# An expert stage rewritten: who rounds the weights, how rows come and go, and where the two choices are summed

## The reference

```
for e in range(N_EXPERTS):
    he = silu(t @ exp_w1[e]) * (t @ exp_w3[e])
    y = y + comb[:, e:e + 1] * (he @ exp_w2[e])
```

## Time and profile before

| | us (or as given) |
|---|---|
| median of 3 runs (3298.52 to 3305.92) | 3304.67 |
| the profiled execution | 3304.96 |
| its span, first to last instruction | 3303.2 |
| DMA traffic | 445.87 MB |
| busy PE / DVE / POOL / ACT | 2738.0 / 1634.0 / 1004.3 / 897.0 |

### The profile page before, as it was taken

The page is one execution under the profiler, slowest core; times in us unless marked ns, Lnnn a source line. Parts: engine busy times, 40 slices in busy tenths (PEclk is TensorE's granted clock), DMA queues, the critical chain, the costliest instruction groups (busy, mean ns, idle before and its releaser), DMA issues. The chain is left out here.

```text
span 3303.2 us, 34922 instructions
## 1 busy us (share of the span) xinstructions
PE 2738.0 (83%) x11986; PEld 2043.3 (62%) x11986; DVE 1634.0 (49%) x1921; ACT 897.0 (27%) x1435; POOL 1004.3 (30%) x743
## 2 busy tenths in 40 slices
PE   5898997999976688619899699979999968588882
PEld 4897555767666566517655355547777757467772
DVE  4394341222134778561166454433564353688884
ACT  3012331000021333230133344422133221234441
POOL 1243222222121656313000233312322211457662
PEclk8898898999987799859799799989999988699996
DMA  2110112111041899864222233221111131699999
GB/s 85 40 45 20 35 27 63 38 51 51 6 154 65 322 339 352 313 219 153 83 58 58 75 81 78 78 63 45 51 39 37 32 136 77 226 361 366 367 356 356
DMA packets 240805, 445.87 MB, mean 135 GB/s; under 512 B 36696, under 2 KB 155816, under 8 KB 232776
## 3 DMA queue, kind: packets, MB, share of 16 engines
q1 hardware_dynamic: 219400, 367.07, 33.2%
q0 software_dynamic: 12960, 47.19, 3.8%
q10 hardware_dynamic: 8352, 30.41, 2.3%
HBM read 349.87 MB, written 90.31 MB: 133 GB/s over the span
## 5 line engine op out<-in xcount | busy, mean ns | idle before, releaser
L1795 DVE TENSOR_TENSOR moe_run_w_low<-moe_run_w,moe_run_w_high 128x2048 fp32r<-128x2048 f32 x174 | 456.0, 2628 | 87.0 <-POOL moe_run_w_high L1655 86.9
L1655 POOL CAST moe_run_w_high<-moe_run_w 128x2048 fp32r<-128x2048 f32 x116 | 285.8, 2471 | 217.5 <-DMA moe_run_w<-w_up 104.4
L134 PE MATMUL rnn_ps<-uT_again_high,rnn_w_high 128*128 128x512 f32 x512 | 205.1, 401 | 35.9 <-POOL rnn_w_low L147 19.9
L134 PE MATMUL rnn_ps<-uT_again_low,rnn_w_high 128*128 128x512 f32 x512 | 202.3, 395 | 0.0
L134 PE MATMUL rnn_ps<-uT_again_high,rnn_w_low 128*128 128x512 f32 x512 | 202.3, 395 | 0.0
L1684 PE MATMUL moe_run_up<-moe_run_w_high,moe_run_xT_high 128*128 128x512 f32 x464 | 199.9, 431 | 0.0
L1684 PE MATMUL moe_run_up<-moe_run_w_low,moe_run_xT_high 128*128 128x512 f32 x464 | 192.4, 415 | 0.0
L1684 PE MATMUL moe_run_up<-moe_run_w_high,moe_run_xT_low 128*128 128x512 f32 x464 | 191.9, 414 | 0.0
L1670 PE MATMUL moe_run_turn<-all_ident,moe_run_x 128*128 128x128 f32 x464 | 78.2, 321 | 131.2 <-DMA moe_run_x<-v,moe_run_idx 131.0
L134 PE MATMUL merge_gates<-uT_high,merge_wg_high 128*128 128x512 f32 x384 | 170.8, 445 | 17.4 <-POOL merge_wg_low L147 17.4
L1200 DVE TENSOR_TENSOR merge_gated<-merge_branch,merge_gate 128x512 f32<-128x512 f32 x48 | 33.2, 691 | 304.0 <-ACT merge_gate L1185 304.0
(11 more groups left out here) (440 smaller groups left out, 6779.5 us busy)
## 6 DMA issues: line engine op xcount, KB each, us to landing
moe_run_w<-exp_w SPq DMA_DIRECT2D x96, 512.0 KB, 8.5
moe_run_w<-w_gate SPq DMA_DIRECT2D x68, 512.0 KB, 7.0
moe_run_w<-w_up SPq DMA_DIRECT2D x68, 512.0 KB, 8.5
moe_run_w<-w_down SPq DMA_DIRECT2D x34, 1024.0 KB, 7.1
moe_y<-moe_run_y ACTq DMA_DIRECT2D x58, 512.0 KB, 7.1
moe_run_w<-exp_w SPq DMA_DIRECT2D x24, 1024.0 KB, 7.7
rnn_raw<-w_in SPq DMA_DIRECT2D x32, 512.0 KB, 3.9
moe_y<-moe_run_zero SPq DMA_DIRECT2D x26, 512.0 KB, 8.2
```

What stands on the lines that cost most here:

```text
L134: last = pe.matmul(out, a, b, start=(k == 0), stop=(k == n - 1))
L1655: pool.tensor_copy(hi[p][j][:], raw[p][j][:]).then_inc(s_hi[j], 1)
L1795: dve.tensor_tensor(lo[p][j][:], raw[p][j][:], hi[p][j][:].bitcast(F32), ALU.subtract).then_inc(s_lo[j], 1)
```

## The change

ACT now rounds w0 and w1 too (`round_up`), so ACT makes all high parts. Its order over block b becomes round_up(b+2, w0), round_middle(b), round_rows(b+2), round_up(b+2, w1), gate(b+1), round_down(b+1), copy_results(b). The first pass is written out, the others loop.

POOL keeps the indirect DMAs alone. It gathers block b+3 as soon as the rows of b+1 are turned, and scatters the results of block b: each result row goes to row (choice x 1024 + token) of `y_d`, which now has 2048 rows. ACT issues no store. Empty places carry an index outside the bounds, in gather and scatter, and those rows are left out; the two row buffers are cleared once at the start, and POOL waits for that before the first gather. The zero fill of unused blocks is gone.

The combination moves into `run_experts`. The tiles of h are loaded into the raw weight tiles of w0 and w1 behind the last blocks, the results are loaded as plain contiguous tiles, all 16 of them into the high and low weight tiles, once both last scatters have landed; sums, norm and stores follow as before. `route_tokens` gains a few small DVE operations and loses `slots`.

```diff
                 for k, oh in enumerate((oh1, oh2)):
...
-                    own(dve.tensor_copy(r["slots"][:, k, :], sl[:]))
...
                     own(TT(of_block[k][:], table(b_id[:], NB), wide(blk[:], NB), ALU.is_equal))
-                    TT(of_block[k][:], of_block[k][:].bitcast(F32), wide(t_id[:], NB), ALU.mult).then_inc(s_hot, 1)
+                    own(TS(sl[:], t_id[:], (k - 2.0) * S, None, ALU.add))
+                    TT(of_block[k][:], of_block[k][:].bitcast(F32), wide(sl[:], NB), ALU.mult).then_inc(s_hot, 1)
...
                 own(dve.tensor_copy(r["passes"][:], pf[:]))
+                own(dve.memset(r["token"][:, NB:], S))
                 dve.wait_ge(s_ids, 1)
-                dve.tensor_copy(r["token"][:], ps_id[:, 0:NB])
+                own(TS(choice[:], ps_id[:, 0:NB], 2.0 * S, None, ALU.add))
+                own(dve.tensor_copy(r["choice"][:], choice[:]))
+                own(TS(second[:], choice[:], float(S), -float(S), ALU.is_ge, ALU.mult))
+                own(TT(choice[:], choice[:], second[:], ALU.add))
+                dve.tensor_copy(r["token"][:, 0:NB], choice[:])
...
         x = [st.sb(f"x{p}", [P, D]) for p in range(2)]
...
+
+        def rows_of(tiles):
...
+        parts = [q.bitcast(F32) for q in rows_of([hi[p][j] for p in range(2) for j in range(3)] + [lo[0][0], lo[0][1]])]
+        yk = [parts[2 * t:2 * t + 2] for t in range(NT)]
         turn, hturn = st.banks("turn", 2), st.ps("hturn")
         up, down = st.banks("up", 2), st.banks("down", 2)
 
...
-                    sp.sem_inc(s_fill, 16)
                 in_order(sp, load)
                 n = more(sp)
-                sp.wait_ge(s_zero, 1)
-                with sp.Fori(n + 1, NB // 2 + 1) as i:
-                    for p in range(2):
-                        sp.dma_start(y_d[bass.ds((2 * i + p) * P, P), :], zero[:]).then_inc(s_fill, 16)
-                sp.wait_ge(s_fill, 16 * (NB + 2))
+                if g_row is not None:
+                    sp.dma_start(g[:], g_row.to_broadcast((P, D))).then_inc(s_g, 16)
+                for t in range(NT):
+                    if t % 2 == 0:
+                        sp.wait_ge(s_lo[t // 2 % 2], 2 * n + 1 + t // 4)
+                    sp.dma_start(h[t], h_d[t * P:(t + 1) * P, :]).then_inc(s_h[t], 16)
+                for p in range(2):
+                    sp.wait_ge(s_st[p], 16 * n + 16)
+                for t in range(NT):
+                    for k in range(2):
+                        at = k * S + t * P
+                        sp.dma_start(yk[t][k], y_d[at:at + P, :]).then_inc(s_yk[t], 16)
+                for t in range(NT):
+                    if g_row is not None:
+                        sp.wait_ge(s_out, t + 1)
+                    else:
+                        sp.wait_ge(s_sum, 2 * t + 2)
+                    sp.dma_start(out_d[t * P:(t + 1) * P, :], h[t]).then_inc(s_kept, 16)
+                sp.wait_ge(s_kept, 16 * NT)
...
             @block.gpsimd
             def _(pool):
-                def gather_and_round(i, p, first):
-                    b = 2 * i + p
-                    if not first:
-                        pool.wait_ge(s_turn, 2 * b - 2)
-                        pool.sem_inc(s_go, 1)
+                def gather(b, p):
                     pool.tensor_copy(idx[p][:], r["token"][:, bass.ds(b, 1)]).then_inc(s_idx, 1)
                     pool.wait_ge(s_idx, b + 1)
                     pool.sem_inc(s_go, 1)
                     pool.indirect_dma_start(
                         out=x[p][:], out_offset=None, in_=v_d,
-                        in_offset=bass.IndirectOffsetOnAxis(ap=idx[p][:, 0:1], axis=0)).then_inc(s_x[p], 16)
-                    for j, s_used in enumerate((s_half, s_up)):
-                        pool.wait_ge(s_raw[p][j], 32 * i + 32)
-                        if not first:
-                            pool.wait_ge(s_used, b - 1)
+                        in_offset=bass.IndirectOffsetOnAxis(ap=idx[p][:, 0:1], axis=0),
+                        bounds_check=S - 1, oob_is_err=False).then_inc(s_x[p], 16)
+
+                def scatter(i, p):
+                    b = 2 * i + p
+                    pool.wait_ge(s_y, 2 * b + 2 + Y0)
+                    pool.sem_inc(s_go, 1)
+                    pool.tensor_copy(to[p][:], r["choice"][:, bass.ds(b, 1)]).then_inc(s_to, 1)
+                    pool.wait_ge(s_to, b + 1)
+                    pool.sem_inc(s_go, 1)
+                    pool.indirect_dma_start(
+                        out=y_d, out_offset=bass.IndirectOffsetOnAxis(ap=to[p][:, 0:1], axis=0),
+                        in_=y[p][:], in_offset=None,
+                        bounds_check=2 * S - 1, oob_is_err=False).then_inc(s_st[p], 16)
+
+                pool.wait_ge(s_clear, 2)
+                gather(0, 0)
+                gather(1, 1)
+                pool.wait_ge(s_turn, 2)
+                gather(2, 0)
+                n = more(pool)
+                with pool.Fori(0, n) as i:
+                    for p in range(2):
+                        b = 2 * i + p + 3
+                        pool.wait_ge(s_turn, 2 * b - 2)
                         pool.sem_inc(s_go, 1)
-                        pool.tensor_copy(hi[p][j][:], raw[p][j][:]).then_inc(s_hi[j], 1)
-                in_order(pool, gather_and_round)
+                        gather(b, 1 - p)
+                        scatter(i, p)
+                for p in range(2):
+                    scatter(n, p)
+                pool.wait_ge(s_x[0], 16 * n + 32)
+                pool.sem_inc(s_go, 1)
...
             @block.scalar
             def _(act):
                 act.sem_inc(s_y, Y0)
-                for p in range(2):
-                    act.sem_inc(s_st[p], ST0)
+
+                def round_up(i, p, j, first=False):
+                    act.wait_ge(s_raw[p][j], 32 * i + 32)
+                    if not first:
+                        act.wait_ge((s_half, s_up)[j], 2 * i + p - 1)
+                    act.copy(hi[p][j][:], raw[p][j][:]).then_inc(s_hi[j], 1)
...
-                def store(i, p):
+                def copy_results(i, p, first=False):
                     b = 2 * i + p
-                    act.wait_ge(s_st[p], 16 * i + ST0)
+                    if not first:
+                        act.wait_ge(s_st[p], 16 * i)
                     for h, (a, z) in enumerate(HALVES):
                         act.wait_ge(s_down, 2 * b + h + 1 + DOWN0)
                         act.copy(y[p][:, a:z], down[h][:]).then_inc(s_y, 1)
-                    act.wait_ge(s_y, 2 * b + 2 + Y0)
-                    act.dma_start(y_d[bass.ds(b * P, P), :], y[p][:]).then_inc(s_st[p], 16)
-
+
+                round_up(0, 0, 0, True)
                 round_rows(0, 0, True)
+                round_up(0, 0, 1, True)
                 round_rows(0, 1, True)
+                round_up(0, 1, 0, True)
+                round_up(0, 1, 1, True)
                 round_down(0, 0, True)
                 gate(0, 0, True)
                 n = more(act)
-                with act.Fori(0, n) as i:
+                def one_pass(i, first=False):
                     for p in range(2):
                         nxt = (i + p, 1 - p)
-                        round_down(*nxt)
+                        round_up(i + 1, p, 0)
                         round_middle(i, p)
                         round_rows(i + 1, p)
+                        round_up(i + 1, p, 1)
                         gate(*nxt)
-                        store(i, p)
+                        round_down(*nxt)
+                        copy_results(i, p, first)
+
+                one_pass(0, True)
+                with act.Fori(1, n) as i:
+                    one_pass(i)
                 round_down(n, 1)
                 round_middle(n, 0)
                 gate(n, 1)
-                store(n, 0)
+                copy_results(n, 0)
                 round_middle(n, 1)
-                store(n, 1)
-                for p in range(2):
-                    act.wait_ge(s_st[p], 16 * n + 16 + ST0)
-                    act.sem_inc(s_end, 1)
+                copy_results(n, 1)
+                if g_row is not None:
+                    for t in range(NT):
+                        act.wait_ge(s_sum, 2 * t + 2)
+                        act.activation(junk[:], h[t], ACT.Square, accum_out=ss[:, t:t + 1]).then_inc(s_ss, 1)
+                        act.wait_ge(s_ms, t + 1)
+                        act.activation(rt[:, t:t + 1], ms[:, t:t + 1], ACT.Sqrt).then_inc(s_rt, 1)
...
-                dve.memset(zero[:], 0.0).then_inc(s_zero, 1)
+                for p in range(2):
+                    dve.memset(x[p][:], 0.0).then_inc(s_clear, 1)
                 rest_of_rows(0, 0)
...
-
-
-def combine(nc, name, r, h_d, y_d, g_row, out_d):
...
-            def _(pool):
-                for t in range(NT):
-                    for k in range(2):
-                        if t >= 2:
-                            pool.wait_ge(s_sum, 2 * (t - 2) + k + 1)
-                        pool.indirect_dma_start(
```

(22 more changed lines are left out.)

57 lines of the change are left out of this document (17 added, 40 removed).

## The result

The changed kernel runs in 3271.67 us (median of four: 3259.74 to 3277.74) against 3303.86 us of the kernel before beside it. The ratio is 0.9893, with a 95% interval of 0.9867 to 0.9919. So 32 us were gained of the 111 forecast. The direction was right, the time lies above the range, and nearly all that is missing is missing in one place, the two expert loops.

The account below looks back on a forecast made before the run. It took stage 2 as a DMA bound loop and stage 1 as nearly one. Gains of 38.6 + 39.3 (periods) + 16 (starts) + 3 + 16 (tails) - 2 (routing) = 111 us gave 3305 - 111 = 3194 us, range 3175 to 3212.

Parts of the forecast that it names:

- the part on the engines: Expert loops: per block ACT 8.86 us, DVE 9.84, POOL 6.9; gather(b+4) wanted more than one period after POOL's wait.
- both period terms: Expert loops: stage 1 from 12.08 to 10.4 us per block gains 38.6 us, stage 2 from 11.39 to 10.2 gains 39.3.
- the prediction's own signs of being wrong: Wrong if ACT's PE waits survive beside its casts, software queue bytes do not fall, or DVE's means rise.
- the floors: DMA time per block at 376 GB/s: 10.2 us stage 1, 9.7 stage 2; 11.15 in both at full traffic.
- the rival in which the landing stays long: Expert loops: weight landing stays 8.5 us, period 10.75 us, 52 us gained there, 3220 us; chance 0.18.
- My 7.4 us for the landing of w_up: Stage 2 loop: w0's second half lands in 7.4 us instead of 8.5, the queue being shorter in proportion to traffic.
- the chain: Expert loops: weight load, landing, ACT casts, DVE low part, 0.7 us hand-overs; two blocks take 20.3 us in stage 2.
- PE as the bound: Expert loops: PE sets a period of 9.52 us in both stages, gaining 121 us there, 3151 us; chance 0.13.
- Empty rows are not saved: Expert loops: left-out rows still cost queue time, period 11.15 us, 29 us gained there, 3243 us; chance 0.11.
- The slower rival: Expert loops: ACT bound by its PE waits, period 12.4 us, 41 us lost against 33 gained, 3313 us; chance 0.04.
- The start: Before each expert loop: both gathers issued at once let products start sooner, 8 us gained per stage, 16 in all.
- The tails: After the expert loops: scatter landing, contiguous loads and sums gain 3 us in stage 1, 16 in stage 2.

Follow-up runs that it names:

- act_only: Kernel before with ACT rounding w0 and w1 in the changed order and POOL only gathering; stores, zero fills and combination as before: 3239.86 us, ratio 0.9784.
- lag_third: Changed kernel with POOL issuing each scatter one gather later, so gathers go ahead; places not dealt: 3203.96 us, ratio 0.9703.
- early: Changed kernel with places dealt over partitions, scatters one gather later, and w2(b+1)'s parts made first in ACT's and DVE's loops: 3199.37 us, ratio 0.9675.
- noskip: Changed kernel with nothing left out: empty places gather a real row and store to spare rows: 3269.47 us.
- lag_noskip: Changed kernel with each scatter one gather later and nothing left out (empty places gather real rows, store to spare rows): 3243.59 us, ratio 0.9824.

## Why the prediction was right and wrong, step by step

**The step that failed** is in the part on the engines: "No POOL wait now holds weights. Behind its wait for the result copy stands gather(b+4), which is wanted more than one period later." The first sentence is true. The second looks at when gather(b+4) is wanted, counted from the wait's beginning, not from its end. The wait lasts until block b's down product is copied out, at the end of block b's work, and gather(b+4) then still needs 4.8 us for scatter(b)'s copy and issue, 1.0 for its own copy and 8.3 us to land. The trace after shows it issued 6 us before PE can turn. "With the gather far ahead" then opened the sum of the period, so both period terms (38.6 and 39.3) stood on it. I had written POOL's order down and summed its busy time (6.9 of 10.4 us), but never laid a scatter and the next gather on one time axis. A queue that is idle 112 us in 300 can still be the one that is late. One of the prediction's own signs of being wrong showed it: ACT's waits for PE survive beside its casts (30.6 us in 300 for the turned rows), and ACT is busy 67 to 74 us of 100, not 85 to 87.

**What bound the kernel before** was also read wrongly. The prediction has stage 2 as a DMA bound loop, with a floor of 11.15 us at full traffic. act_only moves the same 4.19 MB per block in 10.58 us, at 392 GB/s, after the casts of w0 and w1 went from POOL to ACT. So 376 GB/s was the rate of that loop and not a limit of the engines, and behind POOL's queue PE waited 80.7 us for rows in the two loops of the kernel before, and never in act_only. The forecast took the floors only as bounds, so this moved no term of its sum.

**The size with the order mended.** With gathers on time the loops gain 29 + 24 = 53 us (lag_third) instead of 78. The nearest to that is the rival in which the landing stays long: it had 10.75 us for both periods and 3220 us, and the runs of that order show 10.50 to 10.81 us and 3200 to 3211 us. My 7.4 us for the landing of w_up assumed a queue shorter in proportion to the bytes. In a steady stretch of the changed kernel it is longer. SP's timeline after:

```profile
2918.92 0.33 SPq L1649 DMA_DIRECT2D moe_run_w<-w_down  x1
...
2920.54 0.38 SPq L1646 DMA_DIRECT2D moe_run_w<-w_up  x1
...
2941.58 0.33 SPq L1649 DMA_DIRECT2D moe_run_w<-w_down  x1
```

and ACT's, the cast that needed that load:

```profile
2931.07 1.90 ACT L1790 CAST moe_run_w_high<-moe_run_w 128x2048 fp32r<-128x2048 f32 x1 [2.49 <-DMA moe_run_w<-w_up]
```

From SP's first issue at 2918.92 to 2941.58 this is 22.7 us for two blocks: 1.6 us to the second half of w0, 10.5 us of landing, and 10.5 for the casts, the low part and hand-overs, which I had at 1.9 x 3 + 0.4 x 2 + 1.2 + 2.55 + 0.7 = 10.9. So here the chain has the length that its parts give, and its one term from the DMA was 3 us short. No row of before shows the 0.7 us for hand-overs; in this stretch ACT's operations follow one another without a gap, and DVE starts the low part 1.2 us after the cast that it needs. That mending this term alone would have given the period is not shown: in early the chain is shorter and ACT's wait for the load is gone, and the period stayed at 10.3 to 10.4 us by another order. With the rows dealt as well, the periods of 10.60 and 10.07 us come to 34 + 44 = 78 us, the forecast's sum, and the time of 3194.84 us is the forecast's 3194. That agreement is luck: the dealing is no part of the change, outside the loops this kernel gained 42 us against 33 forecast, and its profiled run (3186.13) lies 9 us below its median.

**The other rivals.** PE as the bound (3151, period 9.52): no run had a mean period under 10.07. "Empty rows are not saved" came out in the total of the changed kernel (nothing gained, noskip) and was wrong in its cause: the bytes do leave the queue, the late gathers hid what they give, and with gathers on time they are worth 20 to 33 us. The slower rival, ACT bound by its waits, is refuted by act_only.

**The start.** 4.1 and 8.3 us for 8 and 8. What cut stage 1's share to half was not looked into.

**The tails.** The first sum comes 8.4 us after the last result copy (1389.25 to 1397.65; 11 forecast), and the end 39.1 us after it (3236.12 to 3275.2; 39.5 forecast). SP's first loads of results show the parts:

```profile
1392.66 6.00 SPq L1664 DMA_DIRECT2D moe_run_w_high<-moe_y  x12
...
3239.54 6.48 SPq L1664 DMA_DIRECT2D moe_run_w_high<-moe_y  x12
```

The last scatter is issued and landed 3.4 us after the last result copy, in both stages, where I had 6.5; the loads and stores of stage 2 then take 35.7 us, where I had 33. So the good total is in part two errors that cancel. No row of before shows the 2 and 2.5 us that I added for issue and last landing. Stage 1's tail gained 5.5 us up to the last norm (3 forecast). Of this 3.1 is left at the next expert stage's first load: its routing takes 1.0 us longer, as forecast, and the rest is lost in the part between, which the change doesn't touch.

**DVE** became quicker: 2289 ns for its 128x2048 subtraction against 2549 in the earlier trace rows. The prediction named this and took nothing for it.

**What spoke for the failure beforehand.** The earlier trace rows show 28.5 us in 200 of ACT waiting for turned rows, and the first part of the prediction put it down to gathers stuck in POOL's queue. A new occupant of that queue with a longer wait (the result copy, against the weights) should have been priced as the slower rival: the same wait kept gives the period of before, 12.08 and 11.39, with 33 us gained around it, 3272 us. The median is that number. The profiled run has 34.1 us gained around the loops and 6.1 lost in them, so a part of the agreement is chance, and this is an argument from hindsight.

## What to carry to other kernels

When an in-order queue gets a new instruction that waits, date the instruction behind it: the moment the wait ends, plus everything issued before it, plus its landing, against the moment it is needed. Put what needs only a free buffer ahead of what needs a result; here that order was worth 60 to 70 us, and the whole change without it 32. Look at single intervals beside a mean period: two rhythms in one loop can make kernels look equal that are not. If a loop's share falls on every engine and on the DMA at once after a change, look for the oldest wait in the slowest queue before looking at prices.

## What the runs showed of the hardware

- A left-out row of an indirect DMA saves its bytes, not its packet: 16992 packets with 33.59 MB and with 61.87 MB, 144 for each of the 118 DMAs (60 gathers, 58 scatters). The page of the changed kernel has 6912 more packets under 512 bytes than that of noskip (43224 and 36312), and 118 x 128 - 8192 = 6912 is the number of rows left out. Where such DMAs run together the engines show a full share at a low rate (1.00 at 182 GB/s, 3062 to 3064 us after). At full share the loops run at 365 to 371 GB/s (dealt), 361 to 362 (not dealt), 373/0.98 = 381 in lag_noskip (2860 to 3120 us), and 392/1.01 = 388 in act_only, where nothing is left out and the results are stored in plain DMAs. Why the rate per share falls with left-out rows, and whether the dealing works through an evener load of the 16 engines, stays open: no view used here gives the busy time of single engines.
- act_only held 392 GB/s over 200 us, above the 376 of my floors. The Trainium skill, DMA: Bandwidth & Descriptors, section Specifications, puts HBM traffic of one core at about 358 GB/s; this run disagrees, as the trace of before did. The Trainium skill, Perfetto Trace Analysis, section Roofline, says that a core alone can pull more, bounded by the DMA engines at about 435 GB/s. The trace agrees: over 200 us nothing here is above 392 GB/s, over 10 us the weights reach 413.
- The 128x2048 subtraction on DVE takes 2289 ns without POOL's casts beside it, 2549 with them. The issue of a gather on POOL takes from 1.05 to 2.94 us for the same operation (2900 to 3030 us after); why was not looked into.
- After an idle time of 4.58 us PE's granted clock was at the lower level (0.50) for the turning and about 4 us of products, so that the wait cost 7.3 us instead of 4.6.
